# Half-height index scores, modulation sums landing as columns, a place of its own for the first weights, and row-by-row waits

## The chip, the cores and the metric

The kernel runs on one core of a Trainium2 chip. The metric is device time in microseconds (us) of one execution; a kernel's time is the median of three runs. The engines are TensorE (PE; PEld is its weight load), VectorE (DVE), ScalarE (ACT), GpSimd (POOL) and SyncE (SP), which issues most DMAs.

## The reference, cut to what matters

One layer of a block on x (1024 rows x 1024 features, f32), conditioned by one vector c. What the change touches:

```
mod = einsum('bd,de->be', c, w_ada) + b_ada          # 1024 x 6144
sh1, sc1, gt1, sh2, sc2, gt2 = split(mod, 6)
h = rmsnorm(x, g_norm_mix) * (1 + sc1) + sh1
proj = einsum('bsd,de->bse', h, w_in)                # 1024 x 4688
qa, ka, va, qi, ki, wi, qb, kb, vb, gb = split(proj, ...)
qi = rope(qi as 16 heads x 64); ki = rope(ki, one head of 64)
dots  = einsum('bqhe,bse->bqhs', qi, ki)             # contraction over 64
score = einsum('bqh,bqhs->bqs', wi, relu(dots * 64**-0.5))
sel = top_k(score masked by chunk, 256)
```

Attention over the selected keys, a retention branch, the output projection, a mixture of 32 experts and a final norm follow; they are as they were. The kernel before computes everything in f32 in this part.

## The kernel before

Rows of x are eight tiles of 128 (t), features eight groups of 128 (k).

**Opening.** SP issues, in this order, five small constants, the eight tiles of x, and four DMAs of 2 MB: the columns of w_ada for sc1 (s=0), then for sh1 (s=1), each in two halves of four k. They land in `ada_slot`, which fills the two ring buffers and the place of `qiT`. ACT sums squares, DVE scales the rows (L862), PE transposes them and ACT copies them into `hT`. DVE forms, for each s, the sum over k of w_ada times c (L871, L873: one instruction for each k, 16 in all), still spread over 128 partitions. PE adds up the partitions with a matrix of ones as the stationary operand and the 1024 sums as the moving one, two of 512 columns for each s (L1386): every partition then holds all 1024 totals. DVE picks the totals that belong to its partition by multiplying with the identity and reducing, twice for each s (`own_columns`, L837 to L841). The call for s=0 comes after the twelfth of the sixteen sums, that for s=1 after the last. L882 makes (1 + sc1) * g. Then L888 modulates `hT` in sixteen instructions of 512 columns: eight k for rows 0 to 511, eight for 512 to 1023; only the last k of each half increments `hT_ready`.

**Projection, first part.** `CHUNKS_A` lists qi0, qi1, kiwi (ki and wi, 80 columns), qa, ka, va. Weights go through the two buffers of `ring`, chunk n in buffer n % 2; SP issues chunk 0 only when `mac_done` says that s=0 has left the ring's place. PE computes eight k for each of eight row tiles in a chunk (L1414) and waits for `hT_ready` before each tile of chunk 0. ACT copies results out, DVE rotates, PE transposes (L1398), DVE copies the transposed tile to its place (L915 to L923). For ki, DVE first copies the 64 values behind themselves, so that the transposed tile holds ki in partitions 0 to 63 and once more in 64 to 127; then two copies (L922, L923) put the upper half into `kiBD[0:64, 0]` and the lower into `kiBD[64:128, 1]`, whose rest POOL has set to zero (L512).

**Scores.** For row tiles i = 2 to 7 and 16 heads each (96 units u), PE multiplies `qiT[:, h // 2]`, which holds two heads in its 128 partitions, by `kiBD[:, h % 2]` (L1437): the zeros cancel the other head. K = 128 (i + 1) keys, in pieces of at most 512 columns, go into PSUM banks 2 (u % 3) and the next. ACT writes the relu into one of three buffers R (L681), DVE adds it with its weight to ACC (L956 for the first head of a tile, L958 for the fifteen others, L961 masks). PE waits until the relu three units back has read its banks, ACT until DVE has read R three units back. PE starts the next projection chunk when the last relu is done.

**Later.** The second part of the projection (qa, ka, va) has DVE's top-k pieces (L971 to L977) spread between its rotations by a written-out allowance; the retention projection (L1493), attention, the output projection and the experts follow. The order of each engine's work is fixed in the program; SP works through its DMAs in order.

Of the kernel before, what the change touches and what calls it, by code (L numbers as in the profile page):

```python
# [9 lines left out]
ALU = mybir.AluOpType  # L10
# [101 lines left out]
def block_kernel(nc, x, ccol, pos, w_ada, b_cols, b_gt1, b_sc2, b_sh2, b_gt2, g_cols, g_ffn, g_final, w_in, w_o, w_router,  # L112
                 w_up, w_gate, w_down, const, out):
    ctx = ExitStack()
    with ctx:
# [38 lines left out]
        va = KV[:, 4096:8192].rearrange("p (t c) -> p t c", t=T)  # L154
        kiBD = KV[:, 8192:10240].rearrange("p (h s) -> p h s", h=2)
        xall = KV[:, 0:8192].rearrange("p (t d) -> p t d", t=T)
# [38 lines left out]
        def work(spec):  # L195

            out_, off = {}, 0
            for name, shape in spec:
# [4 lines left out]
                elif len(shape) == 3:  # L203
# [5 lines left out]

        W0 = work([("sq", (D,)), ("mac", (2, D)), ("dg", (512,)), ("ang", (T, 40)), ("k", (T, 40)), ("r", (T, 40)), ("c", (T, 40))])  # L210
        WA = work([("tmp", (3, 512)), ("s1", (128,)), ("s2", (128,)), ("trq", (2, 512)), ("R", (3, 1024))])
        WB = work([("qA", (2, 512)), ("kA", (2, 512)), ("qB", (512,)), ("kB", (512,)), ("v", (2, 512)),
                   ("g", (2, 512)), ("qBD", (4, 2, P)), ("kT", (4, P)), ("st", (4, P)),
# [71 lines left out]
        LATE_SLOT = (0, 1, 2, 0, 2, 0, 2, 0)  # L285
        NU = len(SCORED) * NIH

        def cols_of(i):
# [81 lines left out]
        def _(sp):  # L370
# [6 lines left out]
            for s, part in enumerate((1, 0)):  # L377
                for h in range(2):
                    sp.dma_start(ada_slot[s][:, 4 * h:4 * h + 4], wada_v[:, part, 4 * h:4 * h + 4])\
                        .then_inc(G(f"slot{2 * s + h}"), 16)  # L380


            for n, (_, c0, w) in enumerate(CHUNKS_A):
                if n == 0:
                    sp.wait_ge(G("mac_done"), 1)
                if n >= 2:
                    sp.wait_ge(G("a_proj"), T * (n - 1))
                sp.dma_start(ring[n % 2][:, :, 0:w], win_v[:, :, c0:c0 + w]).then_inc(G(f"ld_w{n % 2}"), 16)
                if n == NA1 + 1:
                    sp.wait_ge(G("sc_ready"), NU)  # L390
                    for k in (2, 3):
                        sp.dma_start(wb[k], win_v[:, :, CHUNKS_B[k][1]:CHUNKS_B[k][1] + 512])\
                            .then_inc(G(f"ld_wb{k}"), 16)
# [111 lines left out]
        def _(pool):  # L505
# [4 lines left out]
            own(nc.gpsimd.memset(ones[:, :], 1.0), G("pool_ones"))  # L510

            own(nc.gpsimd.memset(KV[:, 8192:10240], 0.0), G("pool_zero"))  # L512

# [316 lines left out]
        def _(dve):  # L830
            own = Own(dve, G("dve_step"))
            V = nc.vector

            def own_columns(bank, scratch, at, h, signal):

                s3 = scratch.rearrange("p (k n) -> p k n", k=4)
                own(V.tensor_tensor(s3, PS[:, bank, :].rearrange("p (k n) -> p k n", k=4),  # L837
                                    ident.unsqueeze(1).to_broadcast([P, 4, P]), ALU.mult), signal)
                part = mod[:, at, 4 * h:4 * h + 4]
                own(V.tensor_reduce(part, s3, X_AXIS, ALU.add))  # L840
                own(V.tensor_tensor(part, part, bc[:, at, 4 * h:4 * h + 4], ALU.add))  # L841


# [21 lines left out]
            for n in range(2 * KD):  # L865
                s, k = divmod(n, KD)
                mac = W0["mac"][:, s]
                if n % 4 == 0:
                    dve.wait_ge(G(f"slot{n // 4}"), 16)
                if k == 0:  # L870
                    own(V.tensor_scalar(mac, ada_slot[s][:, k], cc[:, k:k + 1], None, ALU.mult), G("mac_part"))  # L871
                else:
                    own(V.scalar_tensor_tensor(mac, ada_slot[s][:, k], cc[:, k:k + 1], mac, ALU.mult, ALU.add),  # L873
                        G("mac_done") if k == KD - 1 else None)
                if n == KD + 3:
                    dve.wait_ge(G("pe_cols"), 1)
                    for h in range(2):
                        own_columns(h, W0["dg"], 0, h, None)
            dve.wait_ge(G("pe_cols"), 2)
            for h in range(2):  # L880
                own_columns(2 + h, W0["dg"], 1, h, None)
            own(V.scalar_tensor_tensor(mod[:, 0, :], mod[:, 0, :], 1.0, gc[:, :], ALU.add, ALU.mult))  # L882

            dve.wait_ge(G("hT_raw"), T)
            for half in range(2):
                for k in range(KD):
                    part = hT[:, k, 512 * half:512 * half + 512]
                    own.go(V.tensor_scalar(part, part, mod[:, 0, k:k + 1], mod[:, 1, k:k + 1], ALU.mult, ALU.add),  # L888
                           G("hT_ready") if k == KD - 1 else None)

# [16 lines left out]
            def a_evacuate(m):  # L907
# [4 lines left out]
                if name == "qa":  # L912
                    if t >= 2:
                        dve.wait_ge(G(f"st_q{t % 2}"), 16 * (t // 2))
                    ins = V.tensor_copy(WA["trq"][:, t % 2].rearrange("p (j n) -> p j n", j=4), bank)  # L915
                elif name == "ka":
                    ins = V.tensor_copy(kaT[:, :, tile(t)], bank)
                elif name in ("qi0", "qi1"):
                    j = 4 * int(name[2])
                    ins = V.tensor_copy(qiT[:, j:j + 4, tile(t)], bank)  # L920
                else:
                    own.go(V.tensor_copy(kiBD[0:64, 0, tile(t)], bank[0:64, 0]))  # L922
                    ins = V.tensor_copy(kiBD[64:128, 1, tile(t)], bank[64:128, 0])  # L923
                own.go(ins, G("a_evac"))

            dve.wait_ge(G("rope_tab"), 1)
            dve.wait_ge(G("pool_zero"), 1)

# [437 lines left out]
        def _(pe):  # L1366
# [34 lines left out]
            def a_project(chunks):  # L1401
                m = turned.index(chunks[0] * T)
                m0 = m
                for n in chunks:
                    name, _, w = CHUNKS_A[n]
                    pe.wait_ge(G(f"ld_w{n % 2}"), 16 * (n // 2 + 1))
                    for t in range(T):
                        u = n * T + t
                        if n == 0:
                            pe.wait_ge(G("hT_ready"), 1 + t // 4)  # L1410
                        if u >= 4:
                            pe.wait_ge(G("a_copied"), u - 3)
                        for k in range(KD):
                            last = mm(PS[:, u % 4, 0:w], hT[:, k, tile(t)], ring[n % 2][:, k, 0:w], start=(k == 0),  # L1414
                                      stop=(k == KD - 1))
# [14 lines left out]
            for u in range(NU):  # L1430
# [286 lines left out]
```

## Time and profile before

| | us |
|---|---|
| three runs: lowest, median, highest | 1916.6, 1916.66, 1916.66 |
| the profiled execution's own time | 1921.34 |
| its span in the profile | 1919.2 |
| PE busy | 1657.2 (86%) |
| DVE busy | 1389.6 (72%) |
| ACT busy | 724.3 (38%) |
| POOL busy | 170.6 (9%) |

The profile shows one execution. A busy share is an average over stages that have different limits, and a PE that is shown busy need not be at its peak, since matmuls are pipelined. Each f32 matmul of the program appears as two PE records and two PEld records. An operand form such as 128*128 128x512 gives the tile of the array (rows*columns) and the moving operand.

### The profile page before, as it was taken

The page shows a single profiled execution, that of the slowest core. Times are in us where ns is not written, and L with a number is a line of the kernel's source. Part 1 is how long each engine was busy: PE and PEld are TensorE (multiplying, and loading weights), DVE is VectorE, ACT ScalarE, POOL GpSimd, SP SyncE. Part 2 cuts the span into 40 slices and gives each one's busy share as a digit, 9 for nine tenths or more (in the row PEclk, how much of TensorE's full clock was granted, in tenths as well). Part 3 has the DMA queues.
Part 4 walks back from the last instruction along what each step waited for, and adds up shares of the span by engine and source line. Part 5 has one row for each costly group of instructions (what it writes and reads, how often), then busy time and mean ns, then how long its engine had stood idle before and what let it go on. Part 6 is the DMA issues. An engine that isn't in the chain of part 4 may idle for free.

```text
span 1919.2 us, 19711 instructions
## 1 busy us (share of the span) xinstructions
PE 1657.2 (86%) x6542; PEld 1090.3 (57%) x6542; DVE 1389.6 (72%) x1888; ACT 724.3 (38%) x819; POOL 170.6 (9%) x173
## 2 busy tenths in 40 slices
PE   2899999999999999468889998359999999999950
PEld 1346554444445545444555666248888888888840
DVE  6323776899778888886655322559999999999948
ACT  4000563000001001121332333037777777777733
POOL 0000000000111111100000000021101101101015
PEclk8899999999999999689999997669999999999985
DMA  9039202200100000672210101079999999999947
GB/s 363 1 132 377 111 1 88 82 14 36 44 6 6 6 12 6 222 257 99 78 49 17 44 28 44 22 291 423 422 411 414 414 412 415 414 414 411 400 161 257
DMA packets 85358, 355.29 MB, mean 185 GB/s; under 512 B 7984, under 2 KB 12208, under 8 KB 60720
## 3 DMA queue, kind: packets, MB, share of 16 engines
q1 hardware_dynamic: 56496, 268.51, 35.3%
q0 software_dynamic: 11776, 44.04, 6.2%
q10 hardware_dynamic: 17024, 41.95, 5.7%
q8 instruction: 35, 0.57, 0.1%
q14 instruction: 27, 0.22, 0.0%
HBM read 295.75 MB, written 58.72 MB: 185 GB/s over the span
## 4 chain that ended last, share of the span: by engine, by line
PE 45%; DVE 7%; ACT 2%; DMA 2%; issue 1%; POOL 0%; POOLq 0%; DVEq 0%; ACTq 0%
PE PS L1610 9%; PE PS L1612 9%; PE PS L1611 9%; PE PS L1572 5%; PE PS L1526 3%; PE PS L1516 3%; PE PS L1605 1%; PE PS L1546 1%; PE PS L1582 1%; DVE wlo L1295 1%; PE PS L1629 1%; ACT WK L730 1%; DVE WK L994 1%; DVE raw L1354 1%; DVE BIG L994 1%
## 5 line engine op out<-in xcount | busy, mean ns | idle before, releaser
L1295 DVE TENSOR_TENSOR wlo<-raw,whi 128x2048 fp32r<-128x2048 f32 x192 | 436.1, 2287 | 45.5 <-ACT whi L757 45.5
L757 ACT ACTIVATE whi<-raw 128x2048 fp32r<-128x2048 f32 x192 | 363.4, 1911 | 56.5 <-DVE WK L1314 45.6
L1414 PE MATMUL PS<-BIG 128*128 128x512 f32 (+1 forms) x768 | 297.5, 543 | 8.6 <-DVE BIG L888 7.5
L1493 PE MATMUL PS<-BIG 128*128 128x512 f32 x512 | 221.6, 593 | 1.4 <-DMA BIG<-in_w_in 0.7
L1414 PEld LDWEIGHTS PS<-BIG 128*128 128x128 f32 x768 | 134.9, 192 | 150.2 <-issue 148.2
L1610 PE MATMUL PS<-whi,xhi 128*128 128x512 f32 x512 | 203.4, 397 | 7.3 <-DVE wlo L1295 6.5
L1612 PE MATMUL PS<-whi,xlo 128*128 128x512 f32 x512 | 200.5, 392 | 0.0
L1611 PE MATMUL PS<-wlo,xhi 128*128 128x512 f32 x512 | 199.9, 390 | 0.0
L973 DVE MAX8 m<-KV 128x8 f32<-128x384 f32 (+5 forms) x192 | 171.6, 894 | 6.0
L974 DVE MATCH_REPLACE8 KV<-m,KV 128x384 f32<-128x384 f32 (+5 forms) x192 | 168.1, 875 | 0.0
L1493 PEld LDWEIGHTS PS<-BIG 128*128 128x128 f32 x512 | 96.7, 190 | 121.7 <-issue 118.6
L1572 PE MATMUL PS<-BIG,WK 128*128 128x512 f32 x256 | 115.8, 606 | 19.1 <-DVE WK L1171 10.1
L730 ACT ACTIVATE WK<-PS 128x512 f32<-128x512 f32 (+3 forms) x96 | 45.0, 490 | 203.9 <-PE PS L1546 203.3
L668 ACT ACTIVATE WK<-PS 128x512 f32<-128x512 f32 (+1 forms) x40 | 21.0, 525 | 258.2 <-PE PS L1414 258.2
L1437 PE MATMUL PS<-KV,BIG 128*128 128x512 f32 (+3 forms) x320 | 115.5, 524 | 1.0 <-DVE KV L923 1.0
L1610 PEld LDWEIGHTS PS<-whi,xhi 128*128 128x128 f32 x512 | 97.0, 189 | 27.4 <-issue 5.7
L1612 PEld LDWEIGHTS PS<-whi,xlo 128*128 128x128 f32 x512 | 96.5, 188 | 20.6
L1610 PE MATMUL PS<-whi,hhi 128*128 128x512 f32 x256 | 103.3, 403 | 5.1 <-DVE hlo L1306 4.9
L1611 PEld LDWEIGHTS PS<-wlo,xhi 128*128 128x128 f32 x512 | 96.7, 189 | 19.0
L958 DVE SCALAR_TENSOR_TENSOR ACC<-WK,wsc,ACC 128x384 f32<-128x384 f32 (+5 forms) x90 | 85.6, 952 | 24.7 <-ACT WK L681 22.8
L1611 PE MATMUL PS<-wlo,hhi 128*128 128x512 f32 x256 | 100.6, 393 | 0.0
L1612 PE MATMUL PS<-whi,hlo 128*128 128x512 f32 x256 | 100.5, 393 | 0.0
(243 smaller groups left out, 2118.9 us busy)
## 6 DMA issues: line engine op xcount, KB each, us to landing
raw<-in_w_gate SPq DMA_DIRECT2D x64, 1024.0 KB, 7.6
raw<-in_w_up SPq DMA_DIRECT2D x64, 1024.0 KB, 7.7
raw<-in_w_down SPq DMA_DIRECT2D x64, 1024.0 KB, 6.8
y_dram<-zero ACTq DMA_DIRECT2D x8, 3072.0 KB, 14.2
BIG<-in_w_in SPq DMA_DIRECT2D x9, 2048.0 KB, 8.7
BIG<-in_w_ada POOLq DMA_DIRECT2D x8, 2048.0 KB, 9.3
y_dram<-WK ACTq DMA_DIRECT2D x32, 512.0 KB, 7.5
BIG<-in_w_ada SPq DMA_DIRECT2D x4, 2048.0 KB, 20.6
```

Source lines behind the costliest of these rows:

```text
L757: nc.scalar.activation(whi[:, slot], raw[:, q], ACT.Copy).then_inc(G("m_hi"), 1)
L958: own(V.scalar_tensor_tensor(acc, R, wsc[:, i, h:h + 1], acc, ALU.mult, ALU.add), G("sc_acc"))
L973: own(V.max(m8, Wk[:, 0:K]))
L974: own(V.match_replace(Wk[:, 0:K], m8, Wk[:, 0:K], TAKEN))
L1295: V.tensor_tensor(wlo[:, slot], raw[:, q], whi[:, slot].bitcast(F32), ALU.subtract)\
L1414: last = mm(PS[:, u % 4, 0:w], hT[:, k, tile(t)], ring[n % 2][:, k, 0:w], start=(k == 0), stop=(k == KD - 1))
L1437: last = mm(PS[:, 2 * (u % 3) + b, 0:w], qiT[:, h // 2, tile(i)], kiBD[:, h % 2, 512 * b:512 * b + w], start=True, stop=True)
L1493: last = mm(PS[:, k, :], hT[:, d, tile(t)], wb[k][:, d, :], start=(d == 0), stop=(d == KD - 1))
L1572: last = mm(PS[:, 7, :], WC["yT"][:, k, :], wo[:, k, 512 * h:512 * h + 512], start=(k == 0), stop=(k == KD - 1))
L1610: mm(out_, x_hi, w_hi, start=first, stop=False)
L1611: mm(out_, x_hi, w_lo, start=False, stop=False)
L1612: return mm(out_, x_lo, w_hi, start=False, stop=final)
```

## The change

- `kiBD` (2048 columns, half of them zeros) becomes `kiD` (1024 columns) with ki in both halves of the partitions. One copy of 128 partitions fills it for each row tile. POOL's memset of 2048 columns and DVE's wait for it go.
- L1437 contracts 64 rows: `qiT` and `kiD` from partitions 0 to 63 for even heads, 64 to 127 for odd ones. The order of units, the banks and the waits stay.
- L1386: the sums become the stationary operand, 128 columns at a time, and one column of ones the moving one: eight matmuls with one output column each for each s. The totals land in one PSUM bank for each s, each on its own partition. `own_columns` goes; DVE adds the bias to 128x8 in one instruction, and the (1 + sc1) * g instruction moves up, to behind the twelfth sum.
- Chunk 0's weights go into `first_w`, 4096 columns at the end of WK, which nothing else uses at that time. SP issues them right behind w_ada, with no wait. Chunk 1 goes into ring 1 and chunk 2 into ring 0 once `mac_done` is 1; from chunk 3 on the wait is the one of before.
- The last half of w_ada for s=1 comes as two DMAs of two k each, and DVE waits for each.
- Every instruction of L888 increments `hT_ready`, and PE waits for each k of the first tile of each half.

```
-            own(nc.gpsimd.memset(KV[:, 8192:10240], 0.0), G("pool_zero"))
...
+        ADA_PARTS = (((0, 4),), ((4, 8),), ((0, 4),), ((4, 6), (6, 8)))
...
+            sp.dma_start(first_w, win_v[:, :, CHUNKS_A[0][1]:CHUNKS_A[0][1] + 512]).then_inc(G("ld_first_w"), 16)
             for n, (_, c0, w) in enumerate(CHUNKS_A):
                 if n == 0:
+                    continue
+                if n == 1:
                     sp.wait_ge(G("mac_done"), 1)
-                if n >= 2:
+                if n >= 3:
                     sp.wait_ge(G("a_proj"), T * (n - 1))
...
                 if n == KD + 3:
                     dve.wait_ge(G("pe_cols"), 1)
-                    for h in range(2):
-                        own_columns(h, W0["dg"], 0, h, None)
+                    own(V.tensor_tensor(mod[:, 0, :], PS[:, 0, 0:KD], bc[:, 0, :], ALU.add))
+                    own(V.scalar_tensor_tensor(mod[:, 0, :], mod[:, 0, :], 1.0, gc[:, :], ALU.add, ALU.mult))
+            dve.wait_ge(G("hT_raw"), T)
             dve.wait_ge(G("pe_cols"), 2)
-            for h in range(2):
-                own_columns(2 + h, W0["dg"], 1, h, None)
+            own(V.tensor_tensor(mod[:, 1, :], PS[:, 1, 0:KD], bc[:, 1, :], ALU.add))
...
-                           G("hT_ready") if k == KD - 1 else None)
+                           G("hT_ready"))
...
-                    own.go(V.tensor_copy(kiBD[0:64, 0, tile(t)], bank[0:64, 0]))
-                    ins = V.tensor_copy(kiBD[64:128, 1, tile(t)], bank[64:128, 0])
+                    ins = V.tensor_copy(kiD[:, tile(t)], bank[:, 0])
...
-                for h in range(2):
-                    last = mm(PS[:, 2 * s + h, :], ones[:, :], W0["mac"][:, s, 512 * h:512 * h + 512], start=True,
-                              stop=True)
+                for k in range(KD):
+                    last = mm(PS[:, s, k:k + 1], W0["mac"][:, s, P * k:P * k + P], ones[:, 0:1], start=True, stop=True)
...
+                            if n == 0 and t % 4 == 0:
+                                pe.wait_ge(G("hT_ready"), KD * (t // 4) + k + 1)
...
-                    last = mm(PS[:, 2 * (u % 3) + b, 0:w], qiT[:, h // 2, tile(i)], kiBD[:, h % 2, 512 * b:512 * b + w],
-                              start=True, stop=True)
+                    rows = slice(HD * (h % 2), HD * (h % 2) + HD)
+                    last = mm(PS[:, 2 * (u % 3) + b, 0:w], qiT[rows, h // 2, tile(i)],
+                              kiD[rows, 512 * b:512 * b + w], start=True, stop=True)
```

## Rows read from the trace of the kernel before

**Rows 1.** The page's 40 slices of the span: PE's busy tenths and its clock.
```profile
PE   2899999999999999468889998359999999999950
...
PEclk8899999999999999689999997669999999999985
```
**Rows 2.** The page's chain of work that ended last, by engine.
```profile
PE 45%; DVE 7%; ACT 2%; DMA 2%; issue 1%; POOL 0%; POOLq 0%; DVEq 0%; ACTq 0%
```
**Rows 3.** Timeline from 24 to 80 us: start, length, instruction [idle before it, releaser].
```profile
34.94 3.78 PE L1386 MATMUL PS<-WK,ones 128*128 128x512 f32 x4 [4.29 <-DVE WK L873]
...
39.67 0.69 DVE L837 TENSOR_TENSOR WK<-PS,cst 128x512 f32<-128x512 f32 x1
...
42.96 5.25 DVE L873 SCALAR_TENSOR_TENSOR WK<-BIG,cc,WK 128x1024 f32<-128x1024 f32 x4
...
48.26 3.78 PE L1386 MATMUL PS<-WK,ones 128*128 128x512 f32 x4 [9.54 <-DVE WK L873]
49.27 0.34 PEld L1386 LDWEIGHTS PS<-WK,ones 128*128 128x128 f32 x1 [0.52 <-issue]
...
52.15 0.69 DVE L837 TENSOR_TENSOR WK<-PS,cst 128x512 f32<-128x512 f32 x1 [3.94 <-PE PS L1386]
...
55.43 0.17 DVE L882 SCALAR_TENSOR_TENSOR mod<-mod,gc 128x8 f32<-128x8 f32 x1
55.63 7.39 DVE L888 TENSOR_SCALAR BIG<-BIG,mod 128x512 f32<-128x512 f32 x16
...
59.52 16.38 PE L1414 MATMUL PS<-BIG 128*128 128x512 f32 x32 [7.48 <-DVE BIG L888]
```
**Rows 4.** Windows: stretch, length, busy us of the engines, PE clock, DMA share, GB/s.
```profile
50.00:60.00 10.00, 2.52 (x4) 0.84 (x3) 7.61 (x17) 0.00 (x0) 0.00 (x0) 0.50 0.00 1
```
**Rows 5.** DMA view of 0 to 60 us: GB/s in 40 slices of 1.5 us.
```profile
GB/s 0 189 258 282 391 393 421 421 421 415 415 404 412 410 412 410 401 418 412 401 412 410 412 291 195 407 411 391 382 389 386 231 0 0 0 0 0 5 0 0
```
**Rows 6.** Timeline from 183 to 196 us, the end of the kiwi chunk.
```profile
184.24 1.87 PEld L1414 LDWEIGHTS PS<-BIG 128*128 128x128 f32 x16
...
194.88 0.33 PE L1398 MATMUL PS<-cst,WK 128*128 128x128 f32 x1 [1.10 <-DVE WK L937]
...
195.50 0.28 DVE L922 COPY KV<-PS 64x128 f32<-64x128 f32 x1
195.82 0.29 DVE L923 COPY KV<-PS 64x128 f32<-64x128 f32 x1
```
**Rows 7.** Timeline, pieces of 196 to 322 us, the scores.
```profile
196.26 7.09 PE L1437 MATMUL PS<-KV,BIG 128*128 128x384 f32 x16 [1.04 <-DVE KV L923]
...
197.77 0.42 DVE L956 TENSOR_SCALAR ACC<-WK,wsc 128x384 f32<-128x384 f32 x1 [1.66 <-ACT WK L681]
...
202.04 1.27 DVE L958 SCALAR_TENSOR_TENSOR ACC<-WK,wsc,ACC 128x384 f32<-128x384 f32 x2 [0.28 <-ACT WK L681]
...
300.39 0.19 PEld L1437 LDWEIGHTS PS<-KV,BIG 128*128 128x128 f32 x1 [0.24 <-issue]
...
312.82 9.71 PE L1414 MATMUL PS<-BIG 128*128 128x512 f32 x22 [1.11 <-ACT WK L681]
...
314.19 0.23 DVE L961 SCALAR_TENSOR_TENSOR ACC<-cst,ACC 128x64 f32<-128x64 f32 x1
```
**Rows 8.** Groups by line and form, 196 to 316 us: count | busy us, mean ns | idle before.
```profile
L1437 PE MATMUL PS<-KV,BIG 128*128 128x512 f32 x192 | 90.4, 592 | 0.0
L1437 PEld LDWEIGHTS PS<-KV,BIG 128*128 128x128 f32 x320 | 59.0, 192 | 56.9 <-issue 44.8 <-ACT WK L681 3.6
L958 DVE SCALAR_TENSOR_TENSOR ACC<-WK,wsc,ACC 128x1024 f32<-128x1024 f32 x15 | 19.3, 1284 | 7.0 <-ACT WK L681 7.0
L681 ACT ACTIVATE WK<-PS 128x1024 f32<-128x1024 f32 x16 | 16.4, 1024 | 11.2 <-PE PS L1437 11.2
```
**Rows 9.** The page's group of all additions of scores.
```profile
L958 DVE SCALAR_TENSOR_TENSOR ACC<-WK,wsc,ACC 128x384 f32<-128x384 f32 (+5 forms) x90 | 85.6, 952 | 24.7 <-ACT WK L681 22.8
```
**Rows 10.** PE timeline from 420 to 560 us, where the retention projection starts.
```profile
493.48 48.33 PE L1493 MATMUL PS<-BIG 128*128 128x512 f32 x112 [0.74 <-DMA BIG<-in_w_in]
```

More of the change, by code:

```diff
@@ L154, in block_kernel @@
         va = KV[:, 4096:8192].rearrange("p (t c) -> p t c", t=T)
-        kiBD = KV[:, 8192:10240].rearrange("p (h s) -> p h s", h=2)
+        kiD = KV[:, 8192:9216]
         xall = KV[:, 0:8192].rearrange("p (t d) -> p t d", t=T)
@@ L208, in work @@
             return out_
-        W0 = work([("sq", (D,)), ("mac", (2, D)), ("dg", (512,)), ("ang", (T, 40)), ("k", (T, 40)), ("r", (T, 40)), ("c", (T, 40))])
+        W0 = work([("sq", (D,)), ("mac", (2, D)), ("ang", (T, 40)), ("k", (T, 40)), ("r", (T, 40)), ("c", (T, 40))])
         WA = work([("tmp", (3, 512)), ("s1", (128,)), ("s2", (128,)), ("trq", (2, 512)), ("R", (3, 1024))])
+        first_w = WK[:, 5904:10000].rearrange("p (k c) -> p k c", k=KD)
         WB = work([("qA", (2, 512)), ("kA", (2, 512)), ("qB", (512,)), ("kB", (512,)), ("v", (2, 512)),
@@ L286, in block_kernel, with ada_landed @@
         NU = len(SCORED) * NIH
+        ADA_PARTS = (((0, 4),), ((4, 8),), ((0, 4),), ((4, 6), (6, 8)))
+        def ada_landed(part, a):
+            return G("ada_last") if a == 6 else G(f"slot{part}")
         def cols_of(i):
@@ L378, in _ @@
                 for h in range(2):
-                    sp.dma_start(ada_slot[s][:, 4 * h:4 * h + 4], wada_v[:, part, 4 * h:4 * h + 4])\
-                        .then_inc(G(f"slot{2 * s + h}"), 16)
+                    for a, b in ADA_PARTS[2 * s + h]:
+                        sp.dma_start(ada_slot[s][:, a:b], wada_v[:, part, a:b]).then_inc(ada_landed(2 * s + h, a), 16)
+            sp.dma_start(first_w, win_v[:, :, CHUNKS_A[0][1]:CHUNKS_A[0][1] + 512]).then_inc(G("ld_first_w"), 16)
             for n, (_, c0, w) in enumerate(CHUNKS_A):
                 if n == 0:
+                    continue
+                if n == 1:
                     sp.wait_ge(G("mac_done"), 1)
-                if n >= 2:
+                if n >= 3:
                     sp.wait_ge(G("a_proj"), T * (n - 1))
@@ L832, in _ @@
             V = nc.vector
[L834 to L841, printed above, removed]
             dve.wait_ge(G("ld_const"), 16 * 5)
@@ L867, in _ @@
                 mac = W0["mac"][:, s]
-                if n % 4 == 0:
-                    dve.wait_ge(G(f"slot{n // 4}"), 16)
+                if any(a == k for a, _ in ADA_PARTS[n // 4]):
+                    dve.wait_ge(ada_landed(n // 4, k), 16)
                 if k == 0:
@@ L876, in _ @@
                     dve.wait_ge(G("pe_cols"), 1)
-                    for h in range(2):
-                        own_columns(h, W0["dg"], 0, h, None)
+                    own(V.tensor_tensor(mod[:, 0, :], PS[:, 0, 0:KD], bc[:, 0, :], ALU.add))
+                    own(V.scalar_tensor_tensor(mod[:, 0, :], mod[:, 0, :], 1.0, gc[:, :], ALU.add, ALU.mult))
+            dve.wait_ge(G("hT_raw"), T)
             dve.wait_ge(G("pe_cols"), 2)
-            for h in range(2):
-                own_columns(2 + h, W0["dg"], 1, h, None)
-            own(V.scalar_tensor_tensor(mod[:, 0, :], mod[:, 0, :], 1.0, gc[:, :], ALU.add, ALU.mult))
-            dve.wait_ge(G("hT_raw"), T)
+            own(V.tensor_tensor(mod[:, 1, :], PS[:, 1, 0:KD], bc[:, 1, :], ALU.add))
             for half in range(2):
@@ L921, in a_evacuate @@
                 else:
-                    own.go(V.tensor_copy(kiBD[0:64, 0, tile(t)], bank[0:64, 0]))
-                    ins = V.tensor_copy(kiBD[64:128, 1, tile(t)], bank[64:128, 0])
+                    ins = V.tensor_copy(kiD[:, tile(t)], bank[:, 0])
                 own.go(ins, G("a_evac"))
             dve.wait_ge(G("rope_tab"), 1)
-            dve.wait_ge(G("pool_zero"), 1)
             def a_rotate(m):
@@ L1405, in a_project @@
                     name, _, w = CHUNKS_A[n]
-                    pe.wait_ge(G(f"ld_w{n % 2}"), 16 * (n // 2 + 1))
+                    if n == 0:
+                        pe.wait_ge(G("ld_first_w"), 16)
+                    else:
+                        pe.wait_ge(G(f"ld_w{n % 2}"), 16 * ((n + 1) // 2))
+                    weights = ring[n % 2] if n else first_w
                     for t in range(T):
                         u = n * T + t
-                        if n == 0:
-                            pe.wait_ge(G("hT_ready"), 1 + t // 4)
                         if u >= 4:
@@ L1413, in a_project @@
                         for k in range(KD):
-                            last = mm(PS[:, u % 4, 0:w], hT[:, k, tile(t)], ring[n % 2][:, k, 0:w], start=(k == 0),
+                            if n == 0 and t % 4 == 0:
+                                pe.wait_ge(G("hT_ready"), KD * (t // 4) + k + 1)
+                            last = mm(PS[:, u % 4, 0:w], hT[:, k, tile(t)], weights[:, k, 0:w], start=(k == 0),
                                       stop=(k == KD - 1))
```

## The prediction

> **What bounds the kernel now.** I read the slices first. PE is at nine tenths or more from slice 3 to slice 16, so nearly all that the change touches lies in a stretch where TensorE is the limit [rows 1]. The chain of waits follows only the last 57% of the span (its shares add up to that) and is mostly PE [rows 2]; the change lies before it, so I went by the timeline.
>
> The first 60 us are a relay. DVE works on the sums without a pause, PE adds them up while it is cold, DVE picks out columns, modulates eight k, and only then does PE's first projection matmul start, at 59.52 [rows 3]. PE's clock in the last ten of these microseconds is 0.50, the lower level, 1.2 GHz [rows 4].
>
> In the scores (196.26 to 312.82, 116.6 us) PE is the limit. A record of 512 columns starts every 0.43 us (a weight load of 0.19 and 0.24 until the next) [rows 7], 0.84 ns a column. A unit is two records over its K columns: 0.64 us at K = 384, 1.71 at 1024, and over 16 heads and the six widths (4224 columns in all) 16 x 4224 x 2 x 0.84 = 113.5 us, which is the stage. DVE waits 22.8 us for ACT in it, and ACT for PE: 11.2 us at K = 1024 alone [rows 8, 9].
>
> **The opening.** Step by step against the timeline:
>
> 1. PE's sums for s=0 lie beside DVE's s=1 sums. They start at 34.94, and DVE asks for them at 39.67. There is 4.7 us of room.
> 2. The first `own_columns` holds DVE from 39.67 to 42.96, 3.3 us [rows 3]. It is replaced by two 128x8 instructions; one of these took 0.17 [rows 3], with a gap 0.2, so 0.4 in all. Gain 2.9, if w_ada has landed by 40.1. Adding up the GB/s row to slice 24 gives 13.2 MB at 36.0 us, and x, constants and w_ada are 13.2 MB [rows 5]; so it has, with 4 us to spare. If the 2 MB of `first_w` interleaved with w_ada instead of following it, all would land by 41 (2.1 MB at 0.41 MB/us is 5.1 us), a loss of at most 1.
> 3. The last four sums take 5.25 as before and end at 45.3.
> 4. PE's columns for s=1. Before: 3.78, and DVE starts 3.89 after PE [rows 3]. After: eight f32 matmuls, 16 pairs of weight load and a one-column matmul. The trace has none. The nearest rows: 16 pairs with 80 columns took 1.87 at full clock [rows 6]; a cold weight load took 0.34 [rows 3], so at most 16 x 0.34 = 5.4. At 0.50 clock the 1.87 would double to 3.7. I take 3.7 and 0.15 for the end: no gain. Ends: 1.9 faster, 1.7 slower.
> 5. The second `own_columns` and L882, 52.15 to 55.63, 3.5 us, become one 128x8 addition, 0.2. Gain 3.3.
> 6. PE starts after the first L888, not the eighth. One takes 7.39 / 16 = 0.46, so 7 x 0.46 = 3.2 us gained. The other waits cost nothing: a k needs two cold records of about 0.85 on PE and 0.46 on DVE, so the next k is always there. Behind PE's waits stand only the projection's matmuls; nobody else waits for them earlier than before.
> 7. `first_w` lands by 36.0 + 5.1 = 41, needed at 50. Chunks 1 and 2 are issued at 34.9 as today and land behind it, by 47, needed tens of microseconds later. One more DMA on SP's queue before them costs about a microsecond of issue, hidden. POOL's memset goes: POOL then waits for DVE at 17.5 anyway, nothing.
>
> Sum 2.9 + 0 + 3.3 + 3.2 = 9.4; PE starts at about 50.1. The slow first matmuls of the cold PE come earlier but are as many. From there PE runs without a gap until the kiwi chunk's end, so the 9.4 arrive there whole. Bounds: 6.7 (late data 1, slow columns 1.7) to 11.3.
>
> **The end of kiwi.** DVE's last four copies run one after the other behind the last transpose, which ends at 195.2; the last pair is 195.50 to 196.11, and PE starts at 196.26 [rows 6, 7]. With one copy for a tile, of 0.29 (these copies differ in partitions alone, and I take it that 128 cost what 64 do; at worst twice, no gain), the last runs from 195.27 to 195.56. Gain 0.5.
>
> **The scores.** This is the large open term. A 64-row matmul streams the same columns, so one by itself costs what it did. But consecutive units now use different halves of the array's rows, and different PSUM banks. If the halves work side by side, the last record of a unit (both at K up to 512 have just two) lies beside the first of the next. In program order a unit then costs PE two records less one overlap: K = 384 0.32 us instead of 0.64, 512 0.43, 640 1.08 - 0.11 = 0.97 , 768 1.29 - 0.22 = 1.07, 1024 1.72 - 0.43 = 1.29.
>
> Then DVE sets the pace. Its additions are 85.6 us for 90 [rows 9]; two back to back took 1.27 at 0.62, a gap of 0.03 [rows 7], so 88.3. The six first heads (0.42 at K = 384 [rows 7], longer ones in proportion to some 0.75) make 3.5 and six masks of 0.23 1.4, with gaps 5.3. Total 93.6. By the two ends, 0.62 and 1.28, DVE has 0.65 + 1.04 ns for each further column: 0.91 at 640, 1.05 at 768; PE's 0.97 and 1.07 add 16 x 0.08 = 1.3. DVE starts 1.5 after PE [rows 7], so it ends 96.4 after the stage's start, where today it ends at 314.42, 118.2 after. PE restarts 1.6 before DVE's end today; then too, since the last relu waits for the addition three units back. ACT needs 1.02 of 1.31 at K = 1024 [rows 8]. That gives 21.8; at K = 384 all three engines are at 0.64 to 0.65 and regain nothing that is lost, so I take 21.0. Ends: 0 (the halves take turns) and 22; a loss is a rival below.
>
> The Trainium skill's page "TensorE: Matmul & The Clock Gate", Part 3, has this overlap: matmuls on distinct row groups run at once, in program order. By it the stage would gain the 21.0, without it 0. No row of this trace shows a tile under 128 rows.
>
> **Carried on.** The stage after is PE's too: its 112 records before and after 493.48 stand back to back, with a wait of 0.74 for weights whose load starts when the buffer is free and so moves along [rows 10]. I count the gains whole.
>
> **Sum.** 9.4 + 0.5 + 21.0 = 30.9. The profiled execution took 1921.34 (span 1919.2, 2.1 around it), so 1890.4; it stands 4.7 above the median of 1916.66, so the forecast is 1885.8.
>
> **Rivals.**
>
> A. The halves take turns: each matmul costs what it did. For it: nothing here has ever overlapped two matmuls, and each f32 matmul is two passes with a weight load each. Against: disjoint rows, weights and banks, and no waits between neighbours. Time 1916.66 - 9.9 = 1906.8. Chance 0.24.
>
> B. Partial overlap: weight loads or waits on the relu keep some of it away, half of the 21 say: 1896. The relu wait speaks for it (PE may run only three units ahead), the 0.02 us between PE's need and DVE's pace at K = 1024 too. Chance 0.15.
>
> C. Slower: changing halves exposes weight loads. Today 59.0 us of loads lie wholly beside matmuls [rows 8]. If each change of half (95) shows one load of 0.192, +18.2, 1925.0; if all 320 do, +61.4, 1968. It decides from 52 exposed loads, where the 9.9 are used up. Against: a load for idle rows has no reason to wait. Chance 0.06.
>
> The same section of the Trainium skill says that a weight load overlaps running matmuls only where the row group differs. The trace disagrees: here all have one form, 128*128, and loads of 0.19 start every 0.43 while PE is never idle [rows 7, 8]. By that rule the loads would be better hidden after, not worse.
>
> D. The clock falls to 1.2 GHz in the scores because half the rows are idle or PE now waits for DVE. PE's records would take twice as long, and a stage without overlap 113 us more: 2020; with it, at K = 1024 2.58 a unit, 1.5 times today's. For it: PE would idle a little in each unit. Against: gaps would stay below those of the transposes in the attention stage, where slices at eight tenths busy hold nine tenths of clock [rows 1]. Chance 0.03.
>
> E. The overlap comes but DVE or a load further on takes part of it back, more than 5 us, some 1893. Chance 0.04, and within the range.
>
> Forecast as summed: 0.48. The likeliest case's own range is 1881 to 1892 (the columns, the late data, 1 or 2 us of friction). The range that holds eight in ten reaches over B to A: 1881 to 1908; C and D are left out. A measurement of this kernel can tell some 0.2% (3.8 us) from none. Faster by more: the forecast, A, B and E, 0.91; within: 0.02 (C with some 50 loads); slower: 0.07.
>
> **What would show it.** Right: L1386 with x16 records for each s in about 3.7 us; PE's first L1414 at 50.1; L1437 records of 64 rows whose starts for two units lie together, DVE idle before L958 near zero, stage length 95 to 97, and L1414 of qa at about 281 to 283. Wrong: idle time on DVE still at 22 us and a stage of 116 (A); PEld starts of L1437 that follow the end of a matmul (C); a clock below 0.9 between 187 and 282 (D); PE waiting for `first_w` at 50 (step 7).

## The result, and the profile after

The changed kernel took 1890.01 us (median of 4 executions, 1885.95 to 1898.33) against 1916.66 before (1916.6 to 1917.71): ratio 0.9865, 95% interval 0.9836 to 0.9895. Two repeats in later comparisons gave 1887.12 against 1917.85 (0.9846, 0.9824 to 0.9868) and 1894.15 against 1916.04 (0.987, 0.9845 to 0.9895). The forecast was 1885.8, in a range of 1881 to 1908. The profiled execution took 1885.95, with a span of 1884.0; that of before took 1921.34.

First the slices of the page, PE's busy tenths and clock [rows 1]. The stretch at nine tenths is shorter, and the lower clock around the start of attention (slices 16 to 18) is still there.

```profile
PE   3999999999999997578888997379999999999950
...
PEclk8999999999999998689999998589999999999975
```

The timeline of the opening [rows 3]: start, length, instruction, idle time before it and its releaser.

```profile
35.00 3.58 PE L1381 MATMUL PS<-ones,WK 128*128 128x1 f32 x16 [4.08 <-DVE WK L872]
...
39.73 0.17 DVE L876 TENSOR_TENSOR mod<-PS,bc 128x8 f32<-128x8 f32 x1
39.93 0.17 DVE L877 SCALAR_TENSOR_TENSOR mod<-mod,gc 128x8 f32<-128x8 f32 x1
40.13 5.25 DVE L872 SCALAR_TENSOR_TENSOR WK<-BIG,cc,WK 128x1024 f32<-128x1024 f32 x4
45.43 3.49 PEld L1381 LDWEIGHTS PS<-ones,WK 128*128 128x128 f32 x16 [6.94 <-DVE WK L872]
45.43 3.58 PE L1381 MATMUL PS<-ones,WK 128*128 128x1 f32 x16 [6.86 <-DVE WK L872]
49.14 0.17 DVE L880 TENSOR_TENSOR mod<-PS,bc 128x8 f32<-128x8 f32 x1 [3.77 <-PE PS L1381]
49.34 7.39 DVE L885 TENSOR_SCALAR BIG<-BIG,mod 128x512 f32<-128x512 f32 x16
...
50.04 16.24 PE L1412 MATMUL PS<-WK,BIG 128*128 128x512 f32 x32 [1.03 <-DVE BIG L885]
```

PE's first projection matmul starts at 50.04, not 59.52. The two picks shrank from 3.3 and 3.5 us to 0.4 and 0.2; PE's sums as columns take DVE from 45.43 to 49.14, 3.7 us in place of 3.9; and PE starts 0.7 us after L885, not 3.9. The end of the kiwi chunk [rows 6], one copy for a tile:

```profile
185.25 0.68 DVE L919 COPY KV<-PS 128x128 f32<-128x128 f32 x2
...
186.07 7.10 PE L1436 MATMUL PS<-KV,BIG 64*128 64x384 f32 x23 [0.47 <-DVE KV L919]
```

The groups of the scores in the changed kernel (count | busy, mean ns of one | idle before) [rows 8]:

```profile
L1436 PE MATMUL PS<-KV,BIG 64*128 64x512 f32 x192 | 80.8, 632 | 0.0
L1436 PEld LDWEIGHTS PS<-KV,BIG 64*128 64x128 f32 x320 | 47.6, 189 | 43.4 <-issue 26.5 <-ACT WK L689 15.4
...
L953 DVE SCALAR_TENSOR_TENSOR ACC<-WK,wsc,ACC 128x1024 f32<-128x1024 f32 x15 | 19.3, 1285 | 0.5
...
L689 ACT ACTIVATE WK<-PS 128x1024 f32<-128x1024 f32 x16 | 16.4, 1024 | 4.2 <-DVE ACC L953 4.2
```

Two signs that the limit has changed hands: DVE, which idled 7.0 us before its 1024-column additions, idles 0.5; and ACT now waits for DVE (4.2 us), where it waited for PE. A record of 512 columns has become longer (632 ns for 592) and the group's busy time shorter (80.8 for 90.4), which is how overlap looks here. The timeline shows it [rows 7]:

```profile
268.82 13.17 DVE L953 SCALAR_TENSOR_TENSOR ACC<-WK,wsc,ACC 128x1024 f32<-128x1024 f32 x10
269.60 7.62 PE L1436 MATMUL PS<-KV,BIG 64*128 64x512 f32 x22
269.96 0.29 PEld L1436 LDWEIGHTS PS<-KV,BIG 64*128 64x128 f32 x2 [0.17 <-ACT WK L689]
...
270.50 0.19 PEld L1436 LDWEIGHTS PS<-KV,BIG 64*128 64x128 f32 x1 [0.24 <-issue]
270.93 0.19 PEld L1436 LDWEIGHTS PS<-KV,BIG 64*128 64x128 f32 x1 [0.24 <-issue]
271.28 0.29 PEld L1436 LDWEIGHTS PS<-KV,BIG 64*128 64x128 f32 x2 [0.17 <-ACT WK L689]
...
278.13 1.02 ACT L689 ACTIVATE WK<-PS 128x1024 f32<-128x1024 f32 x1 [0.30 <-DVE ACC L953]
...
279.21 7.11 PE L1412 MATMUL PS<-BIG 128*128 128x512 f32 x12 [1.98 <-ACT WK L689]
...
282.03 0.23 DVE L956 SCALAR_TENSOR_TENSOR ACC<-cst,ACC 128x64 f32<-128x64 f32 x1
```

Four weight loads make a unit of K = 1024. Two of them now lie within 0.29 us, the last of one unit and the first of the next, and the pattern repeats every 1.32 us (269.96, 271.28), no longer every 1.71. Ten additions of DVE take 13.17 us, 1.32 each, without a gap. The stage from PE's first score matmul to its first projection matmul went from 116.6 to 93.1 us. DVE's last instruction, the mask at 282.03, ends at 282.26, 96.2 us after PE's first score matmul. PE has by then been back at work for 3.1 us: it waits 1.98 us for the last relu, restarts at 279.21, and then its clock is below full, as the windows show (last columns: PE clock, DMA share, GB/s):

```profile
280.00:290.00 10.00, 10.00 (x20) 4.20 (x19) 3.35 (x8) 0.60 (x1) 0.00 (x0) 0.83 1.01 378
```

The landmarks, each from the timeline or a line's first start: first projection matmul 59.5 and 50.0 (gain 9.5); first score matmul 196.3 and 186.1 (10.2); next projection chunk 312.8 and 279.2 (33.6); retention projection 485.6 and 453.7 (31.9); first attention logits 802.8 and 770.2 (32.6); end 1919.2 and 1884.0 (35.2).

### The profile page after: what moved, and what is told of

It is laid out like the page before. It is cut to its first block, busy times and chain, and to the rows that moved or that the text cites. A ratio compares the mean times of both kernels' runs of the same rounds, so it can differ in the third digit from the quotient of the medians.

```text
span 1884.0 us, 19738 instructions
## 1 busy us (share of the span) xinstructions
PE 1628.3 (86%) x6566; PEld 1078.5 (57%) x6566; DVE 1381.4 (73%) x1870; ACT 723.8 (38%) x819; POOL 169.4 (9%) x172
## 4 chain that ended last, share of the span: by engine, by line
PE 46%; DVE 7%; DMA 2%; ACT 2%; issue 1%; POOL 0%; POOLq 0%; DVEq 0%; ACTq 0%
PE PS L1609 9%; PE PS L1611 9%; PE PS L1610 9%; PE PS L1571 5%; PE PS L1525 3%; PE PS L1515 3%; PE PS L1604 1%; PE PS L1545 1%; PE PS L1581 1%; DVE wlo L1290 1%; ACT WK L738 1%; PE PS L1628 1%; DVE WK L989 1%; DMA WK<-x_dram 1%; DMA BIG<-in_w_ada 0%
## 5 line engine op out<-in xcount | busy, mean ns | idle before, releaser
L1412 PE MATMUL PS<-BIG 128*128 128x512 f32 (+1 forms) x640 | 240.6, 531 | 2.0 <-ACT WK L689 2.0
L1412 PEld LDWEIGHTS PS<-BIG 128*128 128x128 f32 x640 | 110.8, 191 | 114.4 <-issue 111.6
L1492 PEld LDWEIGHTS PS<-BIG 128*128 128x128 f32 x512 | 96.7, 190 | 121.0 <-issue 118.6
L1571 PEld LDWEIGHTS PS<-BIG,WK 128*128 128x128 f32 x256 | 48.6, 195 | 83.6 <-issue 55.6
L1436 PE MATMUL PS<-KV,BIG 64*128 64x512 f32 (+3 forms) x320 | 91.2, 556 | 0.5 <-DVE KV L919 0.5
```

The costliest lines, as they stand in the source:

```text
L1412: last = mm(PS[:, u % 4, 0:w], hT[:, k, tile(t)], weights[:, k, 0:w], start=(k == 0), stop=(k == KD - 1))
L1436: last = mm(PS[:, 2 * (u % 3) + b, 0:w], qiT[rows, h // 2, tile(i)], kiD[rows, 512 * b:512 * b + w], start=True, stop=True)
L1492: last = mm(PS[:, k, :], hT[:, d, tile(t)], wb[k][:, d, :], start=(d == 0), stop=(d == KD - 1))
L1571: last = mm(PS[:, 7, :], WC["yT"][:, k, :], wo[:, k, 512 * h:512 * h + 512], start=(k == 0), stop=(k == KD - 1))
```

## The experiments

Stage lengths below are from PE's first score matmul to the start of its last one: 114.9 us before, 90.6 in the changed kernel. The kernel before, run with them, had medians of 1916.0 to 1917.9 us and went from 1914.8 to 1927.8.

**The changed kernel once more (five executions, then six in another comparison).**

> The changed kernel once more, to see its spread. Theory 1 (the clock): its executions differ by the TensorE clock granted in one stretch after the scores; then the runs fall between 1885 and 1899 us as before, each with its own mean clock (0.929 to 0.935), and the slow ones differ from the profile in the attention stage alone. Theory 2 (the scores): the overlap of the halves itself comes and goes; then the score stage, 93.1 us in the profile of the changed kernel, is 5 us or more longer in a slow execution.

> The changed kernel once more, beside the early-restart kernel: 1887 to 1890 us, a wait of 2.0 us before the first projection matmul after the scores and a clock near 0.8 in the ten microseconds behind it, if nothing else differs.

Measured: 1887.12 us (1885.24 to 1893.53) and 1894.15 us (1885.75 to 1901.66). The profile of the second is the execution of 1901.66. Its scores are those of the first profile (90.6 us), its attention stage is not. Windows of 850 to 950 and 950 to 1050 us and the line of the attention logits (durations min/median/max, first and last start), in the first profile of the changed kernel

```profile
850.00:950.00 100.00, 86.07 (x399) 54.30 (x398) 66.28 (x105) 28.82 (x60) 1.66 (x3) 0.97 0.18 58
950.00:1050.00 100.00, 89.26 (x466) 60.24 (x465) 52.66 (x83) 34.88 (x72) 1.09 (x2) 1.00 0.13 43
```
```profile
L1515 PE MATMUL PS<-KV,BIG x192: 272/592/1201, 770.2 to 1130.4; 128*128 128x512 f32 x96, 128*128 128x128 f32 x32, 128*128 128x256 f32 x32, 128*128 128x384 f32 x32
```

and in that of 1901.66:

```profile
850.00:950.00 100.00, 86.82 (x378) 57.48 (x379) 59.80 (x97) 26.18 (x55) 1.66 (x3) 0.86 0.17 56
950.00:1050.00 100.00, 88.85 (x421) 58.27 (x420) 51.85 (x80) 32.39 (x68) 1.09 (x2) 0.95 0.13 43
```
```profile
L1515 PE MATMUL PS<-KV,BIG x192: 272/592/1201, 770.7 to 1143.9; 128*128 128x512 f32 x96, 128*128 128x128 f32 x32, 128*128 128x256 f32 x32, 128*128 128x384 f32 x32
```

The logits start within 0.5 us of each other and end 13.5 apart, with a clock of 0.86 against 0.97. Nearly all of the 15.7 us between the two executions lies there, in a stage that the change does not touch: theory 1. The clock of a whole execution goes the same way (0.936 at 1885.75 us, 0.927 at 1901.66). What sets the clock's course in one execution stays open. The second median, 1894.15, lies above the 1887 to 1890 expected; the wait of 1.98 us and the clock of 0.83 behind it came as expected.

**The scores alone.** The kernel before with `kiD`, one copy and half-height matmuls, no other edit.

> The kernel before with the half-height scores and the single kiD alone (opening as before). If the gains of the two parts add: the opening as before (first projection matmul at 59.5), score stage 93 us instead of 116.6, so some 24 us off 1916.7: 1893 us. If the overlap is only an accident of what comes before it: score stage above 100 us, 1900 us or more. If the spread between executions comes with the scores, the runs here spread over some 10 us; if it comes with the opening, within 1 us.

Measured: 1894.54 us (1892.49 to 1911.15) against 1917.85; ratio 0.9886 (0.9863 to 0.9909); stage 90.5 us. The part gives its 24 us by itself. The execution of 1911.15 is the profiled one, and its attention logits run over 375.5 us (778.9 to 1154.5) instead of the 360 to 365 of most other profiles: the spread of above.

**The opening alone.** The changed kernel with `kiBD` and its full-height matmuls put back.

> The changed kernel with full-height scores, kiBD and its memset and two copies put back. If the parts add: first projection matmul at 50.0, score stage 116.6 us, 9.5 us off 1916.7: 1907 us. If an earlier opening is given back later: 1912 us or more. Spread: within 1 us if it comes with the scores, some 10 us if with the opening.

Measured: 1911.6 us (1907.95 to 1914.81), ratio 0.9968 (0.9955 to 0.9982), so 3.5 to 8.6 us; first projection matmul at 49.95, stage 113.2 us. At the first logits it is 8.6 us ahead of the kernel before. The medians give 2.3 us less than that; the spread of the later stage hides which is right. The spread itself belongs to neither part: it was 18.7 us with the scores alone, 6.9 with the opening alone, and 6.9 in the kernel before beside them. Together the two parts, 23.3 and 6.3 by their medians, make 29.6; the whole change made 30.7 beside them.

**Same half next to same half.** The changed kernel with the even heads of a row tile first, then the odd ones:

```
+        HEAD = [h for odd in range(2) for h in range(odd, NIH, 2)]
...
-                i, h = FIRST_SCORED + u // NIH, u % NIH
+                i, h = FIRST_SCORED + u // NIH, HEAD[u % NIH]
```

> The changed kernel with the heads of a row tile in another order: the eight even ones, then the eight odd ones, so that a unit's neighbour uses the same half of the array except twice in sixteen units. Work, shapes and waits are the same. Theory (neighbouring units of different halves overlap): the stage goes back to about 113 to 116 us (one unit in eight still overlaps, some 2 us less), total about 1908 us. Rival (64-row matmuls are cheaper by themselves, whatever their neighbour): the stage stays at 93 us, total 1890 us.

Measured: 1914.63 us (1906.65 to 1921.04), stage 120.8 us: not 113 to 116 but worse than full height. The windows of 186 to 231 and 231 to 306 us, and relus of ACT at K = 512 (twice) and 640:

```profile
186.00:231.00 45.00, 44.52 (x79) 21.19 (x80) 23.59 (x38) 18.65 (x35) 0.00 (x0) 0.54 0.24 91
231.00:306.00 75.00, 75.00 (x240) 39.95 (x239) 63.47 (x64) 50.30 (x60) 0.00 (x0) 1.00 0.00 1
```
```profile
221.06 0.60 ACT L690 ACTIVATE WK<-PS 128x512 f32<-128x512 f32 x1 [1.11 <-PE PS L1437]
222.77 0.60 ACT L690 ACTIVATE WK<-PS 128x512 f32<-128x512 f32 x1 [1.11 <-PE PS L1437]
...
230.69 0.70 ACT L690 ACTIVATE WK<-PS 128x640 f32<-128x640 f32 x1 [0.38 <-PE PS L1437]
231.77 0.70 ACT L690 ACTIVATE WK<-PS 128x640 f32<-128x640 f32 x1 [0.38 <-PE PS L1437]
```

Two things are in it. Within eight heads of one half a unit of K = 640 takes 1.08 us (230.69, 231.77), what it takes at full height: a half-height matmul is no cheaper by itself, and the rival falls. And PE, busy 44.5 of 45 us, had a clock of 0.54, so a unit of K = 512 took 1.71 us, twice the 0.85 of full clock. In the changed kernel the clock was low only for a few microseconds of the first tile, and the same 45 us had 0.96:

```profile
186.00:196.00 10.00, 9.93 (x33) 5.78 (x34) 7.43 (x13) 6.57 (x15) 0.00 (x0) 0.83 0.97 378
186.00:231.00 45.00, 44.93 (x165) 23.18 (x166) 40.87 (x57) 34.06 (x56) 0.00 (x0) 0.96 0.22 85
```

The fall near the start of the scores is not the change's doing: the kernel before has it too (0.57 over 197 to 201 us, 1.00 from 201 on). What differs with one-sided work is how long PE stayed low, here until 229 us. What brought it up then stays open. This is one profile; but all ten executions of this order had a mean clock of only 0.923 to 0.930, where those of the changed kernel had 0.927 to 0.936.

**The same, but for the first row tile.**

```
+        HALVES = [h for odd in range(2) for h in range(odd, NIH, 2)]
+        HEAD = list(range(NIH)) + (len(SCORED) - 1) * HALVES
```

> The kernel with even heads first, then odd ones, but for the first row tile, whose heads alternate as in the changed kernel. With even-then-odd heads from the start PE's clock stayed at 0.50 from 187 to about 230 us, though PE had no gap. Theory (work on one half of the array doesn't bring the clock up, but keeps it once it is up): the clock is 1.00 from about 190 on, the first tile takes 10.5 us, and the stage is 113 us or a little less without the slow start. Rival (it lets the clock fall, too): the clock goes to 0.50 again within the next tiles and the stage is 120 us or more.

Measured: 1896.3 us, two executions, stage 101.8 us. The first ten microseconds and the last tiles by windows, and relus at K = 1024:

```profile
186.00:196.00 10.00, 9.52 (x34) 4.80 (x34) 7.82 (x15) 6.70 (x15) 0.00 (x0) 1.00 1.02 398
231.00:290.00 59.00, 57.96 (x170) 29.24 (x168) 49.32 (x45) 39.08 (x43) 0.00 (x0) 1.00 0.00 1
```
```profile
275.15 1.02 ACT L691 ACTIVATE WK<-PS 128x1024 f32<-128x1024 f32 x1 [0.69 <-PE PS L1438]
276.87 2.85 ACT L691 ACTIVATE WK<-PS 128x1024 f32<-128x1024 f32 x3 [0.69 <-PE PS L1438]
280.42 1.02 ACT L691 ACTIVATE WK<-PS 128x1024 f32<-128x1024 f32 x1 [0.69 <-PE PS L1438]
```

Here the clock did not fall at the start of the scores at all (1.00 over 186 to 196 us; two other profiles, of the opening alone and of the ring load below, lack the fall too). It then stayed at 1.00 through half-height work without neighbours, in a stage with hardly a gap on PE. So the second half of the theory, that such work keeps the clock up, is shown; the first half, that the alternating heads bring it up, this run could not test, and it rests on the changed kernel against the order before. But the stage is 11 us shorter than the 113 it expected. The relus say where: one every 1.71 us within a half, and at the change of halves three within 2.85. There more than one record ran beside the other half. By the 11.4 us between this stage and the 113.2 of full height, about one whole unit did at each of the ten changes of the last five row tiles: 1.1 us each, where a unit there takes 0.86 to 1.71. The bound of one overlapped record for a unit, on which the prediction's PE times rest, was too tight.

**Where the opening's gain comes from: three reversals, one execution each.** PE waits for a whole half of `hT` again:

> The changed kernel with PE waiting for all eight k of a half, as before, in place of row by row. By the sum of the prediction PE's first projection matmul starts 3.2 us later than the changed kernel's 50.0 us: 53.3. Rival (the cold PE is fed by DVE anyway and PE would have caught up by the clock rising sooner): the first tile's results are ready at the same time.

Ones stationary again, four matmuls of 512 columns and `own_columns`:

> The changed kernel with the sums over partitions as before (ones stationary, four matmuls of 512 columns, totals picked by own_columns). By the prediction: two picks of 3.3 us against 0.4 and 0.2: 2.9 + 3.1 = 6.0 us, PE's own part equal within 0.3; PE's first projection matmul at 56.1 to 56.4. Rival (the first pick would be hidden by the wait for the last weights of the modulation): 53.2.

Chunk 0 in the ring behind `mac_done` again, the last part of w_ada in one DMA:

> The changed kernel with chunk 0's weights in ring buffer 0 behind mac_done and the last 2 MB of w_ada as one DMA, as before. The DMA is issued at 35 us and 2 MB take 5.1 us at the measured rate, so they land by 42, before the 50 at which PE asks: no difference, first matmul at 50.0. Rival (the place apart is what lets PE start early): PE waits on that DMA, first matmul at 51 or later.

The rows of the first projection matmul, in the kernel with the whole-half wait:

```profile
53.34 7.09 PE L1412 MATMUL PS<-WK,BIG 128*128 128x512 f32 x10 [4.22 <-DVE BIG L885]
```

with rows of ones, where `35.84` is the start of the ninth sum (34.98 in the changed kernel):

```profile
35.84 0.75 DVE L879 TENSOR_SCALAR WK<-BIG,cc 128x1024 f32<-128x1024 f32 x1
...
57.28 3.75 PE L1424 MATMUL PS<-WK,BIG 128*128 128x512 f32 x4 [4.12 <-DVE BIG L896]
```

and with the ring load:

```profile
35.83 0.75 DVE L867 TENSOR_SCALAR WK<-BIG,cc 128x1024 f32<-128x1024 f32 x1
...
50.89 9.39 PE L1406 MATMUL PS<-BIG 128*128 128x512 f32 x15 [1.03 <-DVE BIG L882]
```

In the last two the DVE relay ran 0.86 us late from its first sum on, before any edit acts; the second repeat of the changed kernel, which has no edit, ran 0.8 late as well. Counted from the ninth sum, the first matmul comes after 15.06 us in the changed kernel (34.98 to 50.04), 21.44 with rows of ones and 15.06 with the ring load. So the columns are worth 6.4 us (6.0 expected), the waits row by row 3.2 to 3.3 (3.2), and the place apart and the split DMA, taken back together, nothing, as expected. Their totals, 1891.95, 1890.38 and 1892.98, single executions, cannot tell parts of a few microseconds.

**A version without the wait at the end of the scores.** Instead of the wait for the last relu, in the projection:

```
-            pe.wait_ge(G("sc_relu"), NU)
...
+                        if n == NA1 and t in (0, 2):
+                            pe.wait_ge(G("sc_relu"), NU - (2, 0, 1, 0)[t])
```

> The changed kernel in which PE no longer waits for the last relu before the next projection chunk: its first two row tiles wait for the relu three from the end (which frees their banks), the third for the next to last. In the changed kernel PE idles 2.0 us there and then runs four microseconds at half clock. Theory: PE restarts 1.3 us sooner, the clock holds, and some 3 us are gained up to the retention projection; total 2 to 4 us below the changed kernel, within the spread of its runs. Rival: DVE, which ends the scores 2.8 us after PE's restart, becomes what the rotation waits for, and nothing is gained.

> The early-restart kernel once more, beside the changed kernel on the same chip. If its gain is real: PE restarts less than 0.3 us after the last score matmul and the median is 3 to 6 us below the changed kernel's of this comparison. If the earlier difference was the spread of the attention stage's clock: medians within 1.5 us.

Measured: 1881.25 us (1880.05 to 1888.28), ratio to before 0.9814 (0.9792 to 0.9836), and 1886.5 (1880.65 to 1896.99), 0.985 (0.9822 to 0.9877), in the comparison in which the changed kernel had 1894.15. PE's restart and the window behind it:

```profile
276.67 13.57 PE L1414 MATMUL PS<-BIG 128*128 128x512 f32 x31
```
```profile
280.00:290.00 10.00, 10.00 (x24) 4.37 (x23) 6.85 (x18) 0.60 (x1) 0.00 (x0) 1.00 0.96 359
```

PE has no idle time before the restart, 2.5 us earlier than in the changed kernel, the clock is 1.00, and the retention projection starts at 449.5 and 449.8, against 453.7 and 454.4. Counted from the first score matmul, that is 263.8 us in both profiles, against 267.6 in both of the changed kernel: 3.8 us, of which 2.1 are PE's earlier restart and 1.7 the clock. The profile with the ring load separates the two: it has the same wait of 1.98 us, but a clock of 1.00 over 280 to 290 us, and took 265.4 us (0.6 of the difference lie in the scores, where its clock did not dip either). So the wait is not followed by a slower clock every time. The difference of medians is larger (7.7 us side by side, with 3 to 6 expected), but the intervals of the ratios overlap, so for the total the 3.8 us are what I would claim. By its medians this kernel is the fastest of all here.

**Half height in the attention logits.** The early-restart kernel, and in `query_keys`:

```
+                    rows = slice(HD * (h % 2), HD * (h % 2) + HD)
-                    ... WC["qBD"][i % 2][:, h // 2, h % 2, :], kaT[:, h // 2, 512 * b:512 * b + w] ...
+                    ... WC["qBD"][i % 2][rows, h // 2, h % 2, :], kaT[rows, h // 2, 512 * b:512 * b + w] ...
```

> The early-restart kernel in which the attention logits, too, contract 64 rows: the half of the block-diagonal query tile that isn't zero against the same half of the keys. There a unit's neighbours on PE are transposes and value products of 128 rows, not matmuls of the other half. Theory (the gain is the overlap with a neighbour of the other half): nothing to overlap with, no gain; attention stage as long as in the early-restart kernel within the spread of its clock (374 us from the first logits to the last value product, some 10 us either way). Rival (64-row matmuls are cheaper or free PE earlier by themselves): up to 20 us less in that stage. A loss of 5 us or more would say that going from 128 to 64 rows and back costs something, or that half-height work lets the clock fall.

Measured: 1984.76 us (1965.05 to 1987.01), ratio 1.0356 (1.0338 to 1.0375), some 100 us more than without it. Windows and the line of the logits, in the kernel without the edit,

```profile
850.00:950.00 100.00, 86.06 (x394) 53.43 (x393) 67.19 (x107) 27.86 (x59) 1.09 (x2) 0.98 0.18 58
950.00:1050.00 100.00, 88.36 (x463) 59.61 (x463) 49.96 (x80) 34.87 (x72) 1.08 (x2) 1.00 0.13 43
```

and with it:

```profile
850.00:950.00 100.00, 89.60 (x276) 52.69 (x277) 53.27 (x82) 19.41 (x40) 1.66 (x3) 0.70 0.13 43
950.00:1050.00 100.00, 91.23 (x332) 61.20 (x332) 40.13 (x65) 25.91 (x56) 0.54 (x1) 0.68 0.12 36
```
```profile
L1517 PE MATMUL PS<-KV,BIG x192: 269/631/1219, 765.4 to 1208.6; 64*128 64x512 f32 x96, 64*128 64x128 f32 x32, 64*128 64x256 f32 x32, 64*128 64x384 f32 x32
```

No gain without a neighbour of the other half, as the theory had it, and beyond that the clock fell from 0.98 and 1.00 to 0.70 and 0.68. The logits run over 443 us instead of 360. The traces tell roughly how the 83 us divide. At full clock the record behind one of 512 columns starts after 0.52 us where the number of rows changes, in place of 0.43 without the edit, and the first logit record behind a value product after 0.205 in place of 0.112: 0.09 us for a change. PE goes between the logits and other work 124 times, so by an estimate the changes cost 11 us. The mean clock was 0.75 over 765 to 1209 us, and 0.93 over 765 to 1126 us without the edit: some 170 us more at the lower level, which cost at most 85 if all of PE's work scales with the clock, an estimate too. The clock is therefore the larger part, and the transposes and value products, whose shapes are unchanged, bear it out (value products 339 ns on average, 281 without the edit).

## Why the prediction was right

The forecast's sum was 30.9; the medians gave 26.7, 30.7 and 21.9, the two profiles 35.4. By its steps:

- **The opening, steps 1 to 7**: 9.4 forecast, 9.5 in the profile, and each term stood up to its own experiment (6.4 against 2.9 + 3.3 for the columns, 3.2 against 3.2 for the waits, 0 against 0 for the loads). Step 4, priced between 1.9 and 5.4 us, came at 3.7 from start to DVE, as the doubled row of 1.87 had it.
- **The end of kiwi**: 0.5 forecast, 0.7 measured.
- **The scores**: 21.0 forecast, 23.4 measured. The mechanism, DVE at 1.31 us a unit as the new limit, is what the profile shows (1.32), and DVE ends 96.2 us after the stage's start, 96.4 forecast. Two terms were off. PE's restart was kept at 1.6 us before DVE's end "since the last relu waits for the addition three units back"; but with DVE as the limit two additions and the mask are still to come when the last relu is done, and PE restarts 3.1 us before DVE's end (279.21 against 282.26): 1.4 us more. And the 0.8 us taken off for friction did not show.
- **Luck in it**: the end of DVE fits partly because errors cancel. The 1.3 us added for PE above DVE at K = 640 and 768 are not there (DVE idles 0.5 us before the fifteen additions of each, no more than at 1024); the relus at a change of halves show that about a whole unit can overlap, where the prediction let one record. In their place came 0.6 us of idle DVE in the first row tile, while the clock was low, and 0.5 more in DVE's own instructions and gaps than the 93.6 of the sum.
- **Carried on**: "I count the gains whole" was wrong by 1.7 us. PE, no longer the limit, now runs out of work 1.98 us before the last relu is done, and in this profile pays for it with a slower clock; the early-restart kernel removes both. The prediction had asked what DVE does at the end of the stage, not what PE's clock does there. At the retention projection the excess of the scores and this loss, which partly cancel, give a gain of 31.9 against 30.9 forecast. From there to the 35.2 at the end most of the difference lies in the attention logits, 360.2 us against 363.6, whose length differs as much between executions of one kernel.
- **Rival A** (turns): excluded by the 1.32 us pattern, and by the two even-then-odd orders, which are A and have A's 1.08 us a unit at K = 640 and 1.71 at 1024. **B**: half of the overlap lost: no, DVE idles 0.5 us before all its 1024-column additions together. **C**: no load is exposed in the changed kernel; the two rules of the Trainium skill weighed there, from "TensorE: Matmul & The Clock Gate", Part 3, split: matmuls of different row groups did run at once, as it says; loads of one group beside matmuls of that group are in every profile here, against it.
- **Rival D** (clock) was given 0.03 for reasons that were wrong. It argued from gaps; with hardly any gap the clock stayed low for 40 us when half-height work had no neighbour. Its own sign, a clock below 0.9 between 187 and 282, was seen in ten microseconds (0.83 over 186 to 196) and meant nothing, since the kernel before has the same dip; over the whole stretch it was 0.97. That the changed kernel is on the good side of D was luck as far as the prediction goes: its heads alternate because the order of units was kept. With another head order the change would have been worth 3 us, and in the attention stage it would have cost 100.
- **Rival E** (something later takes back more than 5 us): 1.7 us were taken back.
- The distance between 1885.8 and 1890.0 is within the spread of the attention stage's clock, which moves single executions by up to 16 us.

## What to carry to other kernels

Contracting 64 rows paid here only where the next matmul in PE's order used the other 64 rows (always in another bank; the same bank was not tried). Arrange the order first, then look at who becomes the limit (here DVE, at 1.32 us a unit). Half-height matmuls among full-height ones can cost more than the zeros that they save: 0.09 us for each change of height and, much more, the clock of everything around them. Where totals lie in every partition only to be picked out again, make the data the stationary operand and let them land as a column: 6.4 us here, at no cost on PE.

## What the runs showed of the hardware

- PE at 99% busy with half-height matmuls on one half stayed at the lower clock, 1.2 GHz, for some 40 us (0.54 over 186 to 231 us), while with alternating halves it was back at 2.4 GHz within the first ten (0.83 over 186 to 196 us, 1.00 over 200 to 210 in the changed kernel). Once high, it stayed at 1.00 through half-height work without a neighbour in a dense stage (231 to 290 us), but not in the attention stage (0.70 over 850 to 950 us), where other work lies between.
- At a change of halves PE went beyond the next record: three relus of K = 1024 within 2.85 us, where one every 1.71 us is the pace.
- A change between 128-row and 64-row matmuls, either way, put 0.09 us between two records at full clock (0.52 for 0.43 us behind 512 columns, 0.205 for 0.112 behind 64).
- Sixteen pairs of an f32 weight load and a one-column matmul took 3.58 us at half clock (0.50 over 40 to 50 us), 0.22 each.
